# A gate projection in fp32 as its pieces land, low parts behind the residual sums, logits first, and fourteen homes, in a two-layer decoder trunk

## The reference

```python
def mixer(l, x, ...):
    proj = x @ w_in[l]                 # pool, val, glu, lru, gelu, 3 x 1024 gate columns
    ...                                # y_a (pooling), y_b (conv of width 31, LayerNorm), y_c (RG-LRU)
    gates = sigmoid(u_gate + b_gate[l]).reshape(B, T, 3, D)
    merged = gates[:, :, 0] * y_a + gates[:, :, 1] * y_b + gates[:, :, 2] * y_c
    return merged @ w_out[l]

for l in range(2):
    x = layer_norm(ALPHA * x + mixer(l, x), ln1_g[l], ln1_b[l])
    f = swiglu(x) if l == 0 else moe_swiglu(x)     # dense D_FF 2816; top 2 of 8 experts, D_EXPERT 3584
    x = layer_norm(ALPHA * x + f, ln2_g[l], ln2_b[l])
```

## Time and profile before

| what | value |
| --- | --- |
| median of 3 runs | 1543.12 us (1541.24 to 1543.54) |
| profiled execution, its time | 1543.71 us |
| its span, first to last instruction | 1541.6 us |
| busy: TensorE, VectorE, ScalarE, GpSimd | 1418.2, 1351.8, 1120.2, 106.0 us |
| loaded from HBM | 460.79 MB, 301 GB/s over the span |
| mean granted TensorE clock | 0.976 of full speed |

### The profile page before, as it was taken

The page is one execution under the profiler, slowest core; times in us unless marked ns, Lnnn a source line. Parts: engine busy times, 40 slices in busy tenths (PEclk is TensorE's granted clock), DMA queues, the critical chain, the costliest instruction groups (busy, mean ns, idle before and its releaser), DMA issues.

```text
span 1541.6 us, 41001 instructions
## 1 busy us (share of the span) xinstructions
PE 1418.2 (92%) x17716; PEld 1157.4 (75%) x17716; DVE 1351.8 (88%) x1437; ACT 1120.2 (73%) x1073; POOL 106.0 (7%) x155
## 2 busy tenths in 40 slices
PE   6899899999999989899999999999999888887785
PEld 4788787888877878588777698697788675765563
DVE  3898997546479899789999999999999999999996
ACT  3797665434448776467888788898889888988883
POOL 2031013000043001200000000000000000000001
PEclk9999999999999999999999999999999999999998
DMA  9744374546543436499999999999999999999992
GB/s 300 260 151 138 137 252 165 176 165 232 192 175 137 154 120 222 152 363 379 391 395 406 410 411 399 394 395 402 410 411 407 411 405 412 411 400 411 410 395 107
DMA packets 141205, 464.92 MB, mean 302 GB/s; under 512 B 8086, under 2 KB 10262, under 8 KB 126652
## 3 DMA queue, kind: packets, MB, share of 16 engines
q1 hardware_dynamic: 139100, 457.47, 77.8%
q0 software_dynamic: 1760, 4.50, 1.0%
q10 hardware_dynamic: 160, 0.27, 0.1%
HBM read 460.79 MB, written 2.89 MB: 301 GB/s over the span
## 4 chain that ended last, share of the span: by engine, by line
PE 41%; DVE 30%; issue 15%; ACT 6%; DMA 5%; SPq 1%; POOL 1%; DVEq 0%; ACTq 0%
PE ps L806 12%; PE ps L807 12%; PE ps L808 12%; DVE w_lo L2148 10%; DVE w_lo L2151 5%; DVE w_lo L1623 2%; DMA stage<-in_w_in 2%; DMA xhl<-in_moe_w_gate 2%; ACT w_hi L1554 1%; DVE arena L1754 1%; ACT w_hi L1258 1%; DVE arena L1743 1%; DMA mixer_only<-in_moe_w_up 1%; DVE arena L2164 1%; DVE z L2138 1%
## 5 line engine op out<-in xcount | busy, mean ns | idle before, releaser
L806 PE MATMUL ps<-arena,w_hi 128*128 128x128 f16 (+7 forms) x3952 | 563.9, 214 | 30.5 <-issue 15.1
L807 PE MATMUL ps<-arena,w_hi 128*128 128x128 f16 (+7 forms) x3952 | 563.9, 214 | 17.8 <-issue 17.8
L808 PE MATMUL ps<-arena,w_lo 128*128 128x128 f16 (+7 forms) x3952 | 564.1, 214 | 10.5 <-issue 10.5
L806 PEld LDWEIGHTS ps<-arena,w_hi 128*128 128x128 f16 x3952 | 385.1, 99 | 41.3 <-issue 20.4
L807 PEld LDWEIGHTS ps<-arena,w_hi 128*128 128x128 f16 x3952 | 385.1, 99 | 26.7 <-issue 18.9
L808 PEld LDWEIGHTS ps<-arena,w_lo 128*128 128x128 f16 x3952 | 385.1, 99 | 17.7 <-issue 12.0
L806 PE MATMUL ps<-xhl,w_hi 128*128 128x264 f16 x1184 | 331.5, 280 | 9.1 <-ACT arena L1392 4.2
L807 PE MATMUL ps<-xhl,w_hi 128*128 128x264 f16 x1184 | 331.6, 280 | 0.0
L808 PE MATMUL ps<-xhl,w_lo 128*128 128x264 f16 x1184 | 331.3, 280 | 0.0
L1623 DVE SCALAR_TENSOR_TENSOR w_lo<-stage,w_hi 128x2048 f16<-128x2048 f32 (+1 forms) x100 | 222.0, 2241 | 92.0 <-ACT w_hi L1258 91.7
L1258 ACT ACTIVATE w_hi<-stage 128x2048 f16<-128x2048 f32 (+1 forms) x100 | 183.8, 1854 | 102.3 <-PE ps L808 84.3
(11 more groups left out here) (333 smaller groups left out, 1894.4 us busy)
## 6 DMA issues: line engine op xcount, KB each, us to landing
stage<-in_moe_w_gate SPq DMA_DIRECT2D x56, 1024.0 KB, 10.7
stage<-in_moe_w_up SPq DMA_DIRECT2D x56, 1024.0 KB, 11.8
stage<-in_moe_w_down SPq DMA_DIRECT2D x56, 1024.0 KB, 11.6
stage<-in_w_in SPq DMA_DIRECT2D x44, 1024.0 KB, 5.6
mixer_only<-in_moe_w_up SPq DMA_DIRECT2D x20, 1024.0 KB, 10.5
mixer_only<-in_moe_w_gate SPq DMA_DIRECT2D x20, 1024.0 KB, 11.5
xhl<-in_moe_w_gate SPq DMA_DIRECT2D x16, 1024.0 KB, 11.6
mixer_only<-in_moe_w_down SPq DMA_DIRECT2D x16, 1024.0 KB, 11.3
```

The costliest lines, as they stand in the source:

```text
L806: mm(out, ah, bh, start=start, stop=False, skip_group_check=True)
L807: mm(out, ah, bl, start=False, stop=False, skip_group_check=True)
L808: return mm(out, al, bh, start=False, stop=stop, skip_group_check=True)
```

## The change

1. **One gate projection per mixer in fp32** (`AS_LANDED = (11,)`). The two pieces of step 11 are not split. TensorE multiplies the fp32 piece in its `stage` slot with x in fp32 as soon as it has landed: 32 products, 64 instructions, in place of 96 f16 matmuls. Two high and two low parts per mixer are left out; the slot is loaded again when TensorE has used it (`piece_done`). The sigmoid's scale is 1 instead of 1/64; `split` corrects the counts.
2. **Low parts behind the residual sums** (`LOW_LAST`): that of piece 35 in mixer 0, those of 35 and 36 in mixer 1, are made after the last residual sums instead of before the last four.
3. **Routing:** the eight logits products stand in a row, then two tiles' token transposes, the transposed logits, and the other six tiles'. The idle products before the ranks are 2 instead of 12. The low part of piece 105 (PRE + AHEAD) goes from before the logits' copy to behind the token low parts.
4. **Fourteen homes:** to make room, the constants, the gate parameters and the statistics rows move into `mixer_only`, the per-channel parameters into the arena, and the product SiLU x up is written over SiLU (`h_e = silu_e`), for which ScalarE's SiLU waits for the low part of the chunk before the last one. The order of homes changes too; the last one of the first round is `mixer_only`'s third piece, free once the logits are read. The gains of the last norm are loaded two pieces earlier.

```diff
-RING = 12
+RING = 14
...
+AS_LANDED = (11,)
...
-          (26, 27, 28), (29,), (31, 32, 33, 34), (35, 36)]
+          (26, 27, 28), (29,), (31, 32, 33, 34), ()]
 LOW_LATER = {1: 8, 5: 14, 7: 18, 10: 23, 13: 30}
+
+LOW_LAST = [(35,), (35, 36)]
...
+def as_landed(n):
+    return any(n // 2 * 2 == mixer_piece(l) + 2 * s for l in range(L) for s in AS_LANDED)
+
+
+def split(n):
+
+    return n - sum(as_landed(i) for i in range(min(n, PRE)))
...
+                if n >= SLOTS and as_landed(n - SLOTS):
+                    piece_done(sp, n - SLOTS)
+                elif n >= SLOTS:
+                    sp.wait_ge(S["lo_done"], split(n - SLOTS + 1))
...
             def new_home(m):
 
                 if m < SLOTS:
-                    sp.wait_ge(S["lo_done"], PRE + m - SLOTS + 1)
+                    sp.wait_ge(S["lo_done"], split(PRE + m - SLOTS + 1))
                 elif m == SLOTS:
                     filled(sp, ("so", L - 1))
                 elif m == 9:
+                    sp.wait_ge(S["out_dma"], 16 * 11 * L)
+                elif m == 10:
                     filled(sp, ("mix", L - 1, 15, 3))
-                elif m == 10:
+                elif m == 11:
                     filled(sp, ("msq", 2))
-                elif m == 11:
+                elif m == 12:
                     filled(sp, ("xtok", 2, 1))
                     sp.wait_ge(S["z_start"], KT)
+                elif m == 13:
+                    filled(sp, "logits")
...
-        mixer_only = sb("mixer_only", [P, L * C4 * (NS_ * (CW + PW + LW + 1)) + 3 * C4 * P])
+        mixer_only = sb("mixer_only", [P, 3 * PIECE])
...
+        par_d = held("p (k r) -> p k r", k=KT, r=L * NQ)
+        sp4 = held("p (j l) -> p j l", j=C4, l=L)
+        spt = held("p (i j l) -> p i j l", i=6, j=C4, l=L)
+        sp8n = spt[:, 0]
+        ones_d = held("p (a d) -> p a d", a=1, d=P)[:, 0]
+        ones_b = held("p (a d) -> p a d", a=1, d=P)[:, 0]
+        stat = held("p (i t) -> p i t", i=3, t=T)
+        assert held_at[0] <= 3 * PIECE
...
-            landing, mixer_only[:, 0:PIECE], mixer_only[:, PIECE:2 * PIECE],
-            xhl.rearrange("p i k t -> p (i k t)").bitcast(F32)[:, 0:PIECE],
-            scratch[:, 0:PIECE], x.rearrange("p k t -> p (k t)")[:, 0:PIECE]]
+            mixer_only[:, 0:PIECE], mixer_only[:, PIECE:2 * PIECE], landing[:, 0, :], landing[:, 1, :],
+            xhl.rearrange("p i k t -> p (i k t)").bitcast(F32)[:, 0:PIECE], scratch[:, 0:PIECE],
+            x.rearrange("p k t -> p (k t)")[:, 0:PIECE], mixer_only[:, 2 * PIECE:]]
...
-        h_e = carve([2, 4 * CAP])
+        h_e = silu_e
...
-                    t = mm3(bank(names_[j])[:, 0:T], wh(slot, k, j * P, (j + 1) * P, width),
-                            wl(slot, k, j * P, (j + 1) * P, width), xh[:, kk, :], xl[:, kk, :],
-                            kk == 0, kk == KT - 1)
+                    if piece is None:
+                        t = mm3(bank(names_[j])[:, 0:T], wh(slot, k, j * P, (j + 1) * P, width),
+                                wl(slot, k, j * P, (j + 1) * P, width), xh[:, kk, :], xl[:, kk, :],
+                                kk == 0, kk == KT - 1)
+                    else:
+                        t = mm(bank(names_[j])[:, 0:T], home(piece)[:, k * width + j * P:k * width + (j + 1) * P],
+                               x[:, kk, :], start=(kk == 0), stop=(kk == KT - 1))
...
+                    if s in AS_LANDED and l:
+                        pe.wait_ge(S["x_pool"], 2 * KT)
                     for half in range(2):
                         n = b0 + 2 * s + half
                         slot = n % SLOTS
-                        pe.wait_ge(S["lo_done"], n + 1)
+                        if as_landed(n):
+                            pe.wait_ge(*landed(n))
+                        else:
+                            pe.wait_ge(S["lo_done"], split(n + 1))
...
-                if k == KT - 1:
-                    t.then_inc(full_of("logits_t"), 1)
+            t.then_inc(full_of("logits_t"), 1)
+
+            def token_rows(k):
...
+            token_rows(0)
+            token_rows(1)
...
+            for k in range(2, KT):
+                token_rows(k)
             empty(pe, "ranks")
-            keep_busy(bank("ranks"), 12)
+            keep_busy(bank("ranks"), 2)
...
+                if as_landed(n):
+                    return
...
+                               scale=1.0 if s in AS_LANDED else 1 / WS).then_inc(free_of(name), 1)
...
+                            act.wait_ge(S["e_split"], so_far(at, NC, max(c, 1)))
...
+                for m in LOW_LAST[l]:
+                    lo(b0 + m)
                 norm(2 * l, ("mean", 2 * l), ("msq", 2 * l), WS, l, "ln1_g", "ln1_b")
...
-            lo(PRE + AHEAD)
             filled(dve, "logits_t")
...
             for i in range(3):
                 token_lo(i, 1)
+            lo(PRE + AHEAD)
```

More of the change, by code:

```diff
@@ L273, in trunk_kernel @@
         NORM_IDLE = 23
-        ARENA = 12600
+        ARENA = 13008
         arena = sb("arena", [P, ARENA])
@@ L315, in trunk_kernel @@
         so = carve([C4, 81])
-        so_out_at = at[0]
         so_out = carve([DB])
+        par = carve([C4, L * NR])
         scratch = zsq[:, :, :].rearrange("p k t -> p (k t)")
@@ L360, in trunk_kernel @@
         by_count = carve([4, (NE - 1) ** 2]).rearrange("p a (b c) -> p a b c", b=NE - 1)
-        tok = carve([3, 24])
-        landing = carve([PIECE])
-        assert at[0] <= so_out_at
+        tok = carve([3, 18])
+        landing = carve([2, PIECE])
         HOMES = [stage[:, (PRE + i) % SLOTS, :] for i in range(SLOTS)] + [
-            landing, mixer_only[:, 0:PIECE], mixer_only[:, PIECE:2 * PIECE],
-            xhl.rearrange("p i k t -> p (i k t)").bitcast(F32)[:, 0:PIECE],
-            scratch[:, 0:PIECE], x.rearrange("p k t -> p (k t)")[:, 0:PIECE]]
+            mixer_only[:, 0:PIECE], mixer_only[:, PIECE:2 * PIECE], landing[:, 0, :], landing[:, 1, :],
+            xhl.rearrange("p i k t -> p (i k t)").bitcast(F32)[:, 0:PIECE], scratch[:, 0:PIECE],
+            x.rearrange("p k t -> p (k t)")[:, 0:PIECE], mixer_only[:, 2 * PIECE:]]
         assert len(HOMES) == RING
@@ L889, in stats, with rows_half @@
                         mm(bank(mean)[:, 0:T], ones_d[:, :], zsum, start=False, stop=False, skip_group_check=True)
-            def rows_half(slot, names_, half, width, ready=None, idle=0):
+            def rows_half(slot, names_, half, width, ready=None, idle=0, piece=None):
                 steps = [(j, k) for j in range(len(names_)) for k in range(4)]
@@ L948, in _ @@
                             else:
-                                rows_half(slot, names_, half, 512)
+                                rows_half(slot, names_, half, 512, piece=n if s in AS_LANDED else None)
                         if s in (4, 5) and half == 0:
@@ L1614, in lo @@
             def lo(n):
+                if as_landed(n):
+                    return
                 tiles, width = pre_piece(n)[1:]
                 sl = n % SLOTS
-                dve.wait_ge(S["hi_done"], n + 1)
+                dve.wait_ge(S["hi_done"], split(n + 1))
                 if is_gate_up(n):
```

31 lines of the change are left out of this document (9 added, 22 removed).

## The result

The changed kernel takes 1521.95 us in the median (1519.29 to 1523.53, 4 runs), the kernel before 1542.18 us beside it: a ratio of 0.9867 (95% interval 0.9846 to 0.9888), 20.2 us less. The forecast was 1524.5 us (1518.5 to 1533). The profiled execution has a span of 1520.4 us, 21.2 us less than that of before.

A forecast was written before the change was run, and what follows sets the result against it. TensorE and VectorE bound it in turns, the transfer stream being slower from visit 5. Computing starts 15.2 us earlier (12.6 + 2.65), visit 7 gives up to 3.5: 18.7 us off 1543.1, said as 1524.5 us (range 1518.5 to 1533).

The forecast's parts named there:

- Gate in fp32: Gate projection of each mixer: TensorE's stretch grows to 14.24 us, statistics end 4.5 us earlier in mixer 0, 4.1 in mixer 1.
- (D): Rival: the gate trade yields nothing because another wait takes the place; 8.6 us less gain, 1533 us; chance 0.10.
- (E): Rival: fp32 work of this length is granted only 1.2 GHz, twice the price; end at 1553 us; chance 0.03.
- The term of mixer 1: Low parts moved behind mixer 1's residual sums: norm begins 2.7 us earlier with GpSimd locked out, 5.1 us without the lock.
- I hold it locked out: Mixer 1: GpSimd's last square sum is blocked until VectorE's second low part ends, so it comes at 627.4 us.
- rival (B): GpSimd's sum slips in before the low parts, or routing gives its full 3.4 us: about 1521 us; chance 0.14.
- the unblocked 5.1 us: Mixer 1: gain if GpSimd's last sum is not locked out, the norm beginning behind the low parts at 627.2 us.
- Mixer 0: Only one low part moves behind the sums: gain 1.3 us, lower end 0.7, bounded by TensorE's wait of 1.61 us.
- Routing.: Logits products in a row before the gather: 2.65 us taken of 3.4 us; bounds 0.5 and 3.4.
- The bounds 15.2 to 20.3 us for the stream: Expert visits' transfers: 15.2 us earlier where the stream alone is the limit, 20.3 us while homes are full.
- the whole 3.5 us: VectorE's idle time in visit 7, the last: up to 3.5 us won by more homes, leaving under 1 us idle.
- Rival (C): The two additional homes buy no lead; the end moves by the stream's start alone, 15.2 us: 1528 to 1529 us; chance 0.15.

The follow-up runs named there:

- the old kernel with its copies apart: The kernel before the change, with the copies of old states to the outputs counted by a semaphore of their own: 1537.96 us, ratio 0.9972.

## Why the prediction was right

**Gate in fp32.** Right in mechanism and size: 14.4 us for the stretch where 14.24 were worked out, no wait behind it, full clock, 4.7 and 4.3 us gained where 4.5 and 4.1 were forecast. Undoing it costs 4.0 us in each mixer; against the old kernel with its copies apart, too, mixer 0's gain is 4.1 us, so some 0.6 us of the 4.7 are chance. Rivals (D) and (E) are out.

**Low parts behind the sums.** The term of mixer 1 was mis-sized: 2.7 us forecast, 5.0 measured, 4.1 when it alone was undone. The step that failed is "I hold it locked out": GpSimd won by 0.09 us, as rival (B) had it, so the sum was the unblocked 5.1 us; 0.9 of the 5.0 is the half clock that lasted longer in the kernel before than in the run with the low parts ahead. That GpSimd won was luck, by a margin smaller than anything that the prediction could place. But the step would have failed otherwise too. When GpSimd loses it waits for one low part and not for both, and the norm hides that (49.36 us)., from which I took a lock over two, merge two instructions of another kind: the first (4.64 us) ended behind the second low part, the other, begun during the third, waited for that one alone (2.51 us). The Trainium skill's rule ("SBUF — State Buffer", section "SBUF: two separate sides"), an exclusive lock for one instruction, is the one that the sums of squares bear out, in both directions (2.68 us for GpSimd's, 5.01 us for VectorE's pair); I read it as one over a row of instructions. Why the first scaling waited for two is not shown. Mixer 0 gave 1.8 us, against 1.3, and 1.65 when undone; both are above the 1.61 us that the earlier trace rows were said to set as a bound, and the small rest is not explained.

**Routing.** 2.8 us against 2.65, and 2.4 when undone.

**Homes.** The bounds 15.2 to 20.3 us for the stream rested on a norm 12.6 us earlier; it came 17.6 us earlier, hence x's load too. Redone with 17.6 the bounds are 20.2 and 25.3 us. Computing reached visit 7 20.9 us earlier, so the whole 3.5 us needed a stream 24.4 us earlier; visit 7 ended 23.3 us earlier, gave back 2.4 us, and VectorE is still idle for 1.9 us, where the prediction wanted less than 1. Which part of the two homes' 5.1 us did not come is not shown. With twelve homes visit 7 ended 16.6 us before the old one. Rival (C) is out. The two homes are worth 3.1 us in visit 7 beside the rest of the change.

**What the sum left out.** 0.7 us before the first scan (129.3 to 132.4 us in all profiles) and 1.2 us between norm 1 and the scan are chance, the latter from the wait for the state copies (102.35 us in all three kernels without it, 104.7 to 108.0 with it). The tail of 27.7 against 25.6 us is not explained by the change: in the fourteen profiles it is 23.1 to 31.2 us long, 23.3 in a second profile of the changed kernel itself. What differs is when TensorE ends, 11.0 to 19.4 us behind the last low part; the rest is 11.8 to 12.2 us in all of them. In the first one TensorE's granted clock fell after a wait of 2.03 us (windows of the tail):

```profile
1503.20:1507.80 4.60, 4.57 (x11) 0.84 (x12) 2.09 (x3) 0.00 (x0) 0.00 (x0) 0.53 0.01 4
```

and in the kernel before it did not, after 2.31 us. Two profiles with the old code in the tail gave 25.6 and 25.4 us, which is too few to say that the change has no part in it; that stays open. Visit 7 and tail together are 134.1 us before and 133.9 after: in this profile what visit 7 gave did not reach the end.

So the nearness of the total, 21.2 us in the profile against 18.7, is in part luck: mixer 1's norm gave 2.3 us more than forecast, the stretches of chance before the visits 1.9 us more, the other rows together 1.5 us more, while visit 7 and the tail gave 3.2 us less.

## What to carry to other kernels

Where an engine that splits operands is the bound, a product at full precision on another engine's time can be cheaper than the split one: here 3.6 us of TensorE bought 4.4 us of VectorE and the wait and the half clock behind it. An instruction that nobody waits for soon belongs behind the one that the next engine waits for, even when this fills the same engine with the same work. A semaphore that counts two kinds of transfers makes the reader wait for both: a wait in the timeline on a transfer whose data the waiting engine never touches is worth a look before any reordering.

## What the runs showed of the hardware

- GpSimd beside back-to-back low parts on VectorE: a sum of two SBUF tiles waits for one of them (2.68 us instead of 0.74), a scaling with a per-partition operand for two (4.6 us, the first of the two in the earlier trace rows, instead of 0.48; after the change the first one is as long), though one that began during a single low part waited for that one alone (2.5 us). When GpSimd is first, VectorE's pair of low parts takes 5.01 instead of 4.49 us.
- After TensorE's wait of 5.53 us its clock fell in every profile; after waits of 1.9 to 2.7 us in some of them: at the same place and with the same work before it, the tail's last products ran at 1.2 GHz in one execution and at 2.4 GHz in another. Branch 0's 96 products behind a wait of 2.0 us took 12.6 or 11.0 us, in either mixer. One profile does not show whether filling such a wait helped.
- Many stretches repeat to 0.02 us between profiles (the dense FFN 188.09 to 188.11), so a part of a change can be weighed to a tenth of a microsecond there, although whole executions differ by 4 us. It has to be seen first, by profiles of more than one kernel, that a stretch has one length and not two.
